# Attention in a two-block forward pass: one VectorE copy for the transposed probabilities of both heads

## The reference, cut to what matters

```
memory_attention (twice):   4 heads, 256 keys, no mask
forgetting_attention:      12 heads, causal, 128 queries at a time, kend = q0 + 128 keys
gqa_axial_attention (twice): 8 heads, 512 keys, no mask
  logits = q . k * scale (+ gate terms and mask in the causal one)
  p = softmax(logits);  o = p . v
```

## Time and profile before

| | |
|---|---|
| median of 3 runs | 1871.45 us |
| profiled execution | 1870.95 us |
| its span, first to last instruction | 1869.1 us |
| mean granted clock of TensorE | 0.966 |
| VectorE copies L848 | 72, in 128, 256, 384 and 512 columns |
| ScalarE copies L537 | 72, the same sizes |

### The profile page before, as it was taken

The page is one execution under the profiler, slowest core; times in us unless marked ns, Lnnn a source line. Parts: engine busy times, 40 slices in busy tenths (PEclk is TensorE's granted clock), DMA queues, the critical chain, the costliest instruction groups (busy, mean ns, idle before and its releaser), DMA issues.

```text
span 1869.1 us, 22562 instructions
## 1 busy us (share of the span) xinstructions
PE 1703.4 (91%) x7866; PEld 1310.8 (70%) x7866; DVE 913.7 (49%) x1405; ACT 719.9 (39%) x1165; POOL 743.1 (40%) x403
## 2 busy tenths in 40 slices
PE   4968889999999999888999999998999897999895
PEld 3645667888888877643778888886777556777554
DVE  5999535554430032254266666302474544463544
ACT  4333444444432224155355555322413543313540
POOL 2455533444444533333434444543333332433330
PEclk9989889999999999998999999999999998999997
DMA  4210222332333221200223322333212102222001
GB/s 170 64 50 24 100 66 70 102 100 90 97 107 111 101 90 68 91 1 1 90 69 101 100 90 91 122 102 103 94 57 79 34 24 84 80 67 79 23 12 45
DMA packets 39380, 142.59 MB, mean 76 GB/s; under 512 B 4368, under 2 KB 4368, under 8 KB 38928
## 3 DMA queue, kind: packets, MB, share of 16 engines
q1 hardware_dynamic: 38592, 139.57, 23.0%
q10 hardware_dynamic: 720, 2.10, 0.3%
HBM read 139.55 MB, written 2.10 MB: 76 GB/s over the span
## 4 chain that ended last, share of the span: by engine, by line
PE 77%; issue 9%; DVE 6%; POOL 4%; ACT 3%; POOLq 0%; DVEq 0%; ACTq 0%
PE banks L1157 22%; PE banks L1158 22%; PE banks L1159 22%; POOL w_lo L435 3%; PE banks L1274 3%; PE banks L1258 2%; PE banks L1238 2%; ACT prob L525 1%; PE banks L1216 1%; DVE pt L1144 1%; DVE xs_lo L763 1%; PE banks L1404 1%; PE banks L1417 1%; PE banks L1447 0%; POOL prob L446 0%
## 5 line engine op out<-in xcount | busy, mean ns | idle before, releaser
L435 POOL TENSOR_TENSOR w_lo<-raw,w_hi 128x1024 fp32r<-128x1024 f32 x255 | 659.6, 2598 | 941.8 <-ACT w_hi L483 941.8
L1157 PE MATMUL banks<-xs_hi,w_hi 128*128 128x512 f32 x1592 | 639.2, 402 | 41.0 <-DVE xs_lo L1057 12.9
L1158 PE MATMUL banks<-xs_lo,w_hi 128*128 128x512 f32 x1592 | 627.0, 394 | 0.0
L1159 PE MATMUL banks<-xs_hi,w_lo 128*128 128x512 f32 x1592 | 626.1, 393 | 0.0
L1157 PEld LDWEIGHTS banks<-xs_hi,w_hi 128*128 128x128 f32 x1592 | 303.0, 190 | 122.0 <-issue 47.6
L483 ACT ACTIVATE w_hi<-raw 128x1024 fp32r<-128x1024 f32 x255 | 263.2, 1050 | 267.4 <-PE banks L1159 179.1
L1159 PEld LDWEIGHTS banks<-xs_hi,w_lo 128*128 128x128 f32 x1592 | 303.2, 190 | 64.7
L1158 PEld LDWEIGHTS banks<-xs_lo,w_hi 128*128 128x128 f32 x1592 | 303.8, 191 | 63.2 <-issue 2.4
L446 POOL TENSOR_SCALAR prob<-prob,rinv 128x512 f32<-128x512 f32 (+3 forms) x144 | 83.3, 591 | 144.8 <-DVE rinv L835 144.8
L1157 PE MATMUL banks<-hid_hi,w_hi 128*128 128x512 f32 x352 | 136.9, 389 | 0.0
L1158 PE MATMUL banks<-hid_lo,w_hi 128*128 128x512 f32 x352 | 136.9, 389 | 0.0
(11 more groups left out here) (190 smaller groups left out, 1724.4 us busy)
## 6 DMA issues: line engine op xcount, KB each, us to landing
raw<-wstream SPq DMA_DIRECT2D x255, 512.0 KB, 3.5
x<-xT SPq DMA_DIRECT2D x2, 1024.0 KB, 6.2
out<-x SPq DMA_DIRECT2D x8, 256.0 KB, 2.0
memx<-memT SPq DMA_DIRECT2D x1, 1024.0 KB, 11.1
ws_sb<-wsT ACTq DMA_DIRECT2D x2, 512.0 KB, 3.8
sb_sb<-sbT ACTq DMA_DIRECT2D x2, 256.0 KB, 4.1
rope_sb<-rope ACTq DMA_DIRECT2D x1, 512.0 KB, 5.0
par<-params SPq DMA_DIRECT2D x1, 338.5 KB, 3.1
```

What stands on the lines that cost most here:

```text
L435: nc.gpsimd.tensor_tensor(w_lo[s][:].rearrange("p k c -> p (k c)"), raw[s][:], w_hi[s][:].rearrange("p k c -> p (k c)").bitcast(f32), SUB) ...
L1157: MM(dst, w_hi[slot][:, k, :], hi, start=start, stop=False)
L1158: MM(dst, w_hi[slot][:, k, :], lo, start=False, stop=False)
L1159: return MM(dst, w_lo[slot][:, k, :], hi, start=False, stop=stop)
```

## The change

`pt` becomes one tensor of [128, 2 heads, key tiles, 512] in place of two tensors, at the same total size; `b_t` becomes the two-bank PSUM tensor itself. VectorE's `probs_down` copies both heads in one instruction once both are transposed. ScalarE's `odd_down` and the second semaphore are gone. TensorE waits for the one semaphore before the transposes of either head and before the output.

```diff
-        pt1 = [take(f"pt1_{i}", [P, QT, T]) for i in range(2)]
+        pt1 = take("pt1", [P, 2, QT, T])
...
-        b_t = bank[6:8]
+        b_t = two_banks[3]
...
-                    if 2 <= i <= a.n + 1:
-                        odd_down(a, i - 2)
...
-            def odd_down(a, i):
-
-                p, qt = i // QT, i % QT
-                nt = keys_of(a, qt) // P
-                act.wait_ge(at_t, 2 * (a.i0 + i) + 2)
-                if qt == 0 and a.p0 + p:
-                    act.wait_ge(at_o, 2 * (a.p0 + p))
-                A(a.pt[1][:, 0:nt, qt * P:(qt + 1) * P], b_t[1][:, 0:nt * P].rearrange("p (k q) -> p k q", q=P),
-                  ACT.Copy).then_inc(at_pt_odd, 1)
...
-            def even_down(a, i):
+            def probs_down(a, i):
...
-                dve.wait_ge(at_t, 2 * (a.i0 + i) + 1)
+                dve.wait_ge(at_t, 2 * (a.i0 + i) + 2)
                 if qt == 0 and a.p0 + p:
                     dve.wait_ge(at_o, 2 * (a.p0 + p))
-                V.tensor_copy(a.pt[0][:, 0:nt, qt * P:(qt + 1) * P],
-                              b_t[0][:, 0:nt * P].rearrange("p (k q) -> p k q", q=P)).then_inc(at_pt_even, 1)
+                V.tensor_copy(a.pt[:, :, 0:nt, qt * P:(qt + 1) * P],
+                              b_t[:, :, 0:nt * P].rearrange("p e (k q) -> p e k q", q=P)).then_inc(at_pt, 1)
...
                         if b:
-                            pe.wait_ge(at_pt_odd if e else at_pt_even, b)
+                            pe.wait_ge(at_pt, b)
...
-                    pe.wait_ge(at_pt_even, a.i0 + QT * (p + 1))
-                    pe.wait_ge(at_pt_odd, a.i0 + QT * (p + 1))
+                    pe.wait_ge(at_pt, a.i0 + QT * (p + 1))
```

More of the change, by code:

```diff
@@ L209, in two_blocks @@
         vm0 = take("vm0", [P, 2, TM])
-        pt0 = [take(f"pt0_{i}", [P, 2, T]) for i in range(2)]
+        pt0 = take("pt0", [P, 2, 2, T])
         sqm = [take(f"sqm{i}", [P, TM]) for i in range(2)]
@@ L241, in two_blocks @@
         roped = take("roped", [P, T])
-        pt2 = [take(f"pt2_{i}", [P, QT, T]) for i in range(2)]
+        pt2 = take("pt2", [P, 2, QT, T])
         def o_sb(m):
-            return pt2[m // QT][:, m % QT, :]
+            return pt2[:, m // QT, m % QT, :]
         two_banks = [ctx.enter_context(nc.psum_tensor(f"banks{i}", [P, 2, T], f32)) for i in range(4)]
@@ L304, in two_blocks @@
         at_t = sem("at_t")
-        at_pt_even = sem("at_pt_even")
-        at_pt_odd = sem("at_pt_odd")
+        at_pt = sem("at_pt")
         at_o = sem("at_o")
@@ L836, in attend @@
                     if 2 <= i <= a.n + 1:
-                        even_down(a, i - 2)
+                        probs_down(a, i - 2)
                     if i >= 8 and i % QT == 0 and i // QT - 2 < pairs:
                         hook(i // QT - 2)
-            def even_down(a, i):
+            def probs_down(a, i):
                 p, qt = i // QT, i % QT
                 nt = keys_of(a, qt) // P
-                dve.wait_ge(at_t, 2 * (a.i0 + i) + 1)
+                dve.wait_ge(at_t, 2 * (a.i0 + i) + 2)
                 if qt == 0 and a.p0 + p:
                     dve.wait_ge(at_o, 2 * (a.p0 + p))
-                V.tensor_copy(a.pt[0][:, 0:nt, qt * P:(qt + 1) * P],
-                              b_t[0][:, 0:nt * P].rearrange("p (k q) -> p k q", q=P)).then_inc(at_pt_even, 1)
+                V.tensor_copy(a.pt[:, :, 0:nt, qt * P:(qt + 1) * P],
+                              b_t[:, :, 0:nt * P].rearrange("p e (k q) -> p e k q", q=P)).then_inc(at_pt, 1)
             def out_low(a, no):
@@ L1255, in transposes @@
                         if b:
-                            pe.wait_ge(at_pt_odd if e else at_pt_even, b)
+                            pe.wait_ge(at_pt, b)
                         for k in range(keys_of(a, i % QT) // P):
-                            last = nc.tensor.transpose(b_t[e][:, k * P:(k + 1) * P],
+                            last = nc.tensor.transpose(b_t[:, e, k * P:(k + 1) * P],
                                                        prob[b % 2][:, e, k * P:(k + 1) * P], ident)
@@ L1273, in output @@
                         for e in range(2):
-                            last = MM(b_o[n % 2][half(e), q0:T], a.v_of(2 * p + e, k), a.pt[e][:, k, q0:T],
+                            last = MM(b_o[n % 2][half(e), q0:T], a.v_of(2 * p + e, k), a.pt[:, e, k, q0:T],
                                       start=(k == 0), stop=(k == nt - 1))
```

## The result

The changed kernel takes 1888.95 us (median of 4 runs, 1888.32 to 1892.6); the kernel before, beside it, 1872.55. The ratio is 1.0087, 95% interval [1.0064, 1.011]. The direction and the mechanism are those of the prediction; the size is not: 16.4 us instead of 10.3, and the time lies just above the range (1888.0). The kernel before has a fourth run here (1877.38), so its median is 1.1 above the 1871.45 that the forecast was counted from. The profiled execution took 1888.55, its span is 1886.7, 17.6 longer than that of before, and the mean granted clock fell from 0.966 to 0.961.

What follows compares the result with a forecast made beforehand. TensorE is busy 91%, mostly in untouched matmul stages; a loop through scores, maximum, reciprocal, POOL and transposes bounds GQA attention at 2.3 us per block. GQA 8.0 + causal 1.7 + memory 0.6 = 10.3 more gave 1881.7 us, range 1873.5 to 1888.

Steps and rivals of the forecast that it cites:

- a hand-over of 2.39 per block: GQA, single-buffered banks: copy 1.20, 0.08 to transposes, 0.42 first head, 0.69 to next copy; 2.39 us against 2.3 today.
- VectorE's own 2.34: GQA: VectorE's issue alone per block, 1.14 + 0.07 + 1.13 = 2.34 us, longer than today's loop of 2.3.
- The hand-over, 0.08: From the copy's end to the next transposes: 0.08 us, within bounds 0.06 to 0.12.
- First groups, 0.44 twice: First group of blocks in each of two GQA stages: 11.87 us instead of 11.43, 0.44 more.
- Full cycles, 0.75 and 1.04, 1.05, 1.05: GQA cycles of four blocks: 0.75 more, 1.04 in the second layer's first; 1.05 each with the second hook.
- Last groups, 1.63 twice: Last group of each GQA stage, without further scores: output product at 8.81 instead of 7.18 us, 1.63 more.
- Causal, 1.7: Causal attention: 0.5 for the first cycle, 0.1 in each of four, 0.8 for the last; together 1.7 us.
- Memory, 0.6: Two memory attention stretches: loop covers the copy except at the last block, 0.3 us each, together 0.6.
- TensorE's clock: Rival: added waits lower the granted clock; two or three output products at half clock make 1888 us; chance 0.06.
- ScalarE's relief: Rival, faster: exp starts right after the maximum, scores no longer wait after output products; 5 us won, 1866.5; chance 0.08.
- Larger cover: Rival, no change: per-block increments of 0.1 to 0.3 vanish, only the ends remain, about 3 us: 1874; chance 0.12.
- Two start-ups: Rival: the two-bank copy takes 1.35 instead of 1.20 us, 6 us more in all: 1888; chance 0.09.

Runs made afterwards that it cites:

- waits alone: Kernel before with the change's joint waits, each engine still copying its own bank: 1873.6 us, ratio 1.0003.
- one head: Changed kernel with all its waits, copying only the first head's bank, whose probabilities serve both heads' outputs: 1870.72 us, ratio 0.9987.
- the run with two copies: Kernel before with ScalarE's copy moved to VectorE as a second one-bank copy with its own wait and semaphore: 1880.47 us, ratio 1.0041.
- the pair with all stages filled: Kernel before and changed kernel, each with unread TensorE products in all five attention stages, also behind each last output product: 1886.96 and 1899.13 us.
- The later filled pairs: Both kernels with unread products at the head and last two blocks of GQA stages (1873.18, 1885.24 us), then in all five attention stages (1886.96, 1899.13).
- the first, at 15.9: Both kernels with three unread TensorE products at the head of each GQA stage: before 1872.63 us, changed 1888.51 us.

## Where the prediction was right, and which steps failed

*What was right.* The direction, and the longer copy as the cause (waits alone: nothing; one head: nothing left of the loss). The prediction had both ways in which it costs, a hand-over of 2.39 per block and VectorE's own 2.34, and the run with two copies shows that both pay. The copy's length (1.20, measured 1.219), the engine's cadence (1.13, measured 1.14), the releaser (T's waits name the copy), and the full cycle with two hooks (14.61, measured 14.63) came out. The Trainium skill (Perfetto Trace Analysis, Optimizing Scalar/DVE Operations) led to 1.19 for that cadence; the trace has 1.14, so the row was the better guide. The same section of the Trainium skill says that breaking instructions up may finish work sooner where Vector is not saturated but causes bubbles on other engines. In direction the runs agree: two copies are some 8 us faster than one. In the full cycles, where VectorE has no idle time, they gained least (0.28 and 0.26, in the last group 0.83).

*Terms of the sum that were mis-sized.*
- **The hand-over, 0.08.** From copy start to transposes the trace has 1.37, that is 1.22 and 0.15; the walk had 1.28. That makes 2.47 per block instead of 2.39. It cost 0.23 in a full cycle (14.03 for 13.80), and next to nothing where both hooks stand on VectorE (14.63 for 14.61). The row for it was in my own list, with 0.12 ("0.67 <-DVE pt L848"), and I took less.
- **First groups, 0.44 twice.** At a granted clock of 1.00 on both sides, 17.03 against 16.25 and 16.28: 0.77 each.
- **Full cycles, 0.75 and 1.04, 1.05, 1.05.** O to O: 14.03 - 13.04 and 14.03 - 12.76 = 0.99 and 1.27; 14.63 - 13.56 = 1.07, twice.
- **Last groups, 1.63 twice.** 8.91 - 7.18 = 1.73. GQA at full clock: 9.4, forecast 8.0.
- **Causal, 1.7.** First 0.69 for 0.5; cycles 0.18 for 0.1 (11.46 against 11.28); last 1.35 for 0.8, of which 0.46 is half clock in the last transposes:

```profile
861.72 1.52 PE L1245 MATMUL banks<-cst,prob 128*128 128x128 f32 x8 [1.14 <-DVE pt L835]
...
864.55 4.54 PE L1260 MATMUL banks<-pt,vf 128*64 128x512 f32 x16 [1.32 <-DVE pt L835]
```

So 2.3 at full clock. Memory, 0.6: at a granted clock near 1.00 (the pair with all stages filled) 0.47 + 0.17 = 0.64 in memory 0 (without the products the second term is about 0.25), and I take the same for memory 1, whose own rows differ in clock. The loops come to 9.4 + 2.3 + 1.3 = 13.0 instead of 10.3. This is the first step that failed: of the 2.7, 1.4 lie in GQA (0.7 in the first groups, 0.5 in the full cycles, 0.2 in the last groups), 0.6 in causal and 0.7 in memory attention, where the prediction had POOL cover the copy up to the last block and its first group paid 0.47. The later filled pairs, at 12.1 and 12.2 (about 13.3 without the products' own cost), agree with 13.0; the first, at 15.9, doesn't tell it from the unfilled 16.4.

The larger loops alone would not have left the range: 1871.45 + 13.0 is 1884.5. Another 1.1 is the median of before, which the forecast took from three runs.

*The rest, 3 to 4 us, and the second step that failed: the sum ends at the attention loops.* It puts TensorE's clock and the stretches between the stages at nothing; the clock is only a rival, at odds of 0.06, priced as two or three O at half clock. The runs showed both moving by microseconds, and this is what carried the time over the range. The clock's falls came in another shape than that rival's: in this profile at the head of both GQA stages (18.21 for 17.03 at 1.00 in the first; in the second 19.41 for 17.03, while before lost 17.68 for 16.28 there), at the causal stage's last transposes and O (4.47 for 4.00 before), and in stretches between stages. There the traces differ by 2.8 us with the same code, and in places by clock, as from 655 to 665 us (0.66, before 0.83). It also goes the other way: memory 1's last O fell from 3.61 to 1.86. What is shown: such falls exist, cost 1 to 3.5 us each at the head of a GQA stage, and land elsewhere from kernel to kernel and between two profiles of the changed kernel. What stays open: that they make up the whole rest. The two later filled pairs point to it and the first does not, and all their differences are uncertain by 3 us and more, so that 14 to 16 is not excluded. The runs' own clocks give an estimate: over 77 runs of the kernel before, a mean granted clock higher by 0.001 goes with 0.9 us less, and by that slope the eight runs of the changed kernel lie 14 us above before at equal clock, so that some 2 to 3 us go with the clock.

*Rivals.* ScalarE's relief: S never waits for exp any more, and it does not matter, because the copy now sets the loop. Larger cover: excluded, every cycle paid. Two start-ups (1888, the nearest in time): excluded by 1.219; a right figure for a wrong reason.

## What to carry to other kernels

Where PSUM banks are single-buffered between TensorE and a copier, the time per bank from full to free is in the loop: two banks emptied by two engines, or by two instructions with their own semaphores, let TensorE refill the first while the second drains; one instruction over both takes that away. The copier's own time per block counts beside it (here 16 us for one instruction, 8 for two on the same engine, nothing for two engines). Count a hand-over from copy's end to the next matmul with the dearest row that the trace has. And when a change of under 1% is summed from cycles, put several microseconds on TensorE's clock and on the unchanged stretches, in both directions, and compare the shares of stages at equal granted clock and from more than one profile.

## What the runs showed of the hardware

- A two-bank copy of 1024 fp32 columns from PSUM took VectorE 1.219 us and ScalarE 1.024; of one bank 0.674 to 0.682 and 0.598. ScalarE is the faster copier per column here.
- Products of no use, put in to hold TensorE's clock, brought no gain that the measurement can tell from none (the best, 1.0061 where the change without them has 1.0083 and 1.0087, with overlapping intervals); the fall tended to move to the next quiet place, and with all stages filled a higher mean clock (0.971) went with 15 us more.
- The same instructions between the attention stages took 2.8 us more in the changed kernel's profile than in that of before, and in the stretch between the GQA stages alone about 4 us more again in a second profile of the changed kernel.
